# One block of meta rows, values on both halves of a bank, and other engine orders at a handover in a hybrid decoder kernel

## What is computed

```python
p = rms_norm(x, norm_w) @ w_in          # columns: attention q|k|v|gate, HGRN q|f|i|gate
att = sink_attention(qa, [meta k; window k; new k], [meta v; window v; new v], mask, sinks)
S, o = hgrn_chunk(S0, silu(qh), (1-lb)*sigmoid(-fh), ih, log(lb+(1-lb)*sigmoid(fh)))
y = x + concat([att * silu(ga), rms_norm(o) * silu(gh)]) @ w_out
# sample attention, all in one softmax with a sink column:
keys = concat([meta_k (8,16,2,64), buf_k (8,128,2,64), k])      # per sequence its own 16 meta rows
vals = concat([meta_v, buf_v, v])
```

## Time and profile before

| | us |
|---|---|
| median of 3 runs | 1149.72 (1148.98 to 1150.73) |
| the profiled execution | 1151.39 |
| its span, first to last instruction | 1149.5 |
| TensorE busy | 1117.0 |
| VectorE / ScalarE / GpSimd busy | 712.8 / 438.5 / 360.8 |
| TensorE busy in 550 to 560, 560 to 570 | 8.30, 7.40 of 10 |

### The profile page before, as it was taken

The page is one execution under the profiler, slowest core; times in us unless marked ns, Lnnn a source line. Parts: engine busy times, 40 slices in busy tenths (PEclk is TensorE's granted clock), DMA queues, the critical chain, the costliest instruction groups (busy, mean ns, idle before and its releaser), DMA issues.

```text
span 1149.5 us, 25865 instructions
## 1 busy us (share of the span) xinstructions
PE 1117.0 (97%) x9394; PEld 919.2 (80%) x9394; DVE 712.8 (62%) x1849; ACT 438.5 (38%) x1258; POOL 360.8 (31%) x421
## 2 busy tenths in 40 slices
PE   6999999999999999999889999999999999999998
PEld 4877888888888888888676888888888887678887
DVE  6657666666666666667864556655665666755443
ACT  6402222222222222224323565655576665523320
POOL 0003333333333333333531223322332236532331
PEclk9989999999999999999998999999999999999999
DMA  8531111111111111106331611121111134434431
GB/s 286 183 111 57 66 66 64 64 55 64 64 64 64 64 64 64 45 26 242 109 102 39 230 46 55 50 78 46 56 68 63 46 110 159 144 147 152 151 136 74
DMA packets 49391, 108.33 MB, mean 94 GB/s; under 512 B 5088, under 2 KB 17888, under 8 KB 49312
## 3 DMA queue, kind: packets, MB, share of 16 engines
q1 hardware_dynamic: 49328, 107.51, 26.2%
HBM read 70.23 MB, written 38.26 MB: 94 GB/s over the span
## 4 chain that ended last, share of the span: by engine, by line
PE 86%; DVE 6%; POOL 4%; issue 2%; ACT 1%; DMA 1%; DVEq 0%; SPq 0%; POOLq 0%; ACTq 0%
PE h_bank_b L919 5%; PE h_bank_a L919 5%; PE h_bank_b L921 5%; PE h_bank_b L920 5%; PE h_bank_a L921 5%; PE h_bank_a L920 5%; PE o_bank L2641 4%; PE o_bank L2643 4%; PE o_bank L2642 4%; PE h_bank_t L903 4%; PE a_bank_b L1917 3%; PE a_bank_b L1919 3%; PE a_bank_b L1918 3%; PE a_bank_a L1917 3%; PE a_bank_a L1919 3%; PE a_bank_a L1918 3%
## 5 line engine op out<-in xcount | busy, mean ns | idle before, releaser
L1705 DVE CUSTOM_DVE_ANT_0 a_sm<-a_sc,a_hidden,a_neg_sink 128x272 f32<-128x272 f32 x128 | 57.7, 488 | 83.5 <-PE a_sc L1946 83.4
L919 PE MATMUL h_bank_b<-h_w_hi,h_h_hi 128*128 128x512 f32 x256 | 106.4, 416 | 0.1
L919 PE MATMUL h_bank_a<-h_w_hi,h_h_hi 128*128 128x512 f32 x256 | 103.1, 403 | 0.0
L921 PE MATMUL h_bank_b<-h_w_hi,h_h_lo 128*128 128x512 f32 x256 | 100.8, 394 | 0.0
L920 PE MATMUL h_bank_b<-h_w_lo,h_h_hi 128*128 128x512 f32 x256 | 100.2, 391 | 0.0
L921 PE MATMUL h_bank_a<-h_w_hi,h_h_lo 128*128 128x512 f32 x256 | 99.9, 390 | 0.0
L920 PE MATMUL h_bank_a<-h_w_lo,h_h_hi 128*128 128x512 f32 x256 | 99.7, 389 | 0.0
L1917 PE MATMUL a_bank_a<-a_w_hi,a_h_hi 128*128 128x512 f32 (+1 forms) x208 | 77.5, 373 | 0.5 <-DMA a_h_lo<-h_split 0.5
L1917 PE MATMUL a_bank_b<-a_w_hi,a_h_hi 128*128 128x512 f32 (+1 forms) x200 | 76.3, 382 | 0.0
L1501 ACT ACTIVATE a_prb<-a_sm,a_neg_m 128x256 f32<-128x256 f32 x128 | 64.2, 502 | 27.7 <-DVE a_neg_m L1705 25.8
L1919 PE MATMUL a_bank_a<-a_w_hi,a_h_lo 128*128 128x512 f32 (+1 forms) x208 | 73.6, 354 | 0.0
(11 more groups left out here) (328 smaller groups left out, 3048.4 us busy)
## 6 DMA issues: line engine op xcount, KB each, us to landing
h_split<-h_h_hi SPq DMA_DIRECT2D x17, 512.0 KB, 3.0
h_split<-h_h_lo SPq DMA_DIRECT2D x17, 512.0 KB, 3.8
a_h_hi<-h_split SPq DMA_DIRECT2D x17, 512.0 KB, 3.5
a_h_lo<-h_split SPq DMA_DIRECT2D x17, 512.0 KB, 4.4
h_x<-x_prompt SPq DMA_DIRECT2D x16, 512.0 KB, 3.4
o_m<-mixed SPq DMA_DIRECT2D x16, 512.0 KB, 4.1
o_x<-x_prompt SPq DMA_DIRECT2D x16, 512.0 KB, 4.3
y_prompt<-o_x SPq DMA_DIRECT2D x16, 512.0 KB, 2.6
```

The costliest lines, as they stand in the source:

```text
L919: pe.matmul(out[:, :], h_hi[t.slot][:, k, :], hi, start=(k == 0), stop=False)
L921: ins = pe.matmul(out[:, :], h_lo[t.slot][:, k, :], hi, start=False, stop=(k == KT - 1))
L1705: ins = dve.tensor_tensor_reduce(SM[j % 2][:, i, :], sc[:, i, 0:KEYS], hidden[:, mask, :], -SCALE, neg_sink[:, h:h + 1], ALU.add, ALU.min, ...
```

## The change

Five things are changed. The meta keys and values of all 8 sequences are loaded as one block of 128 rows; one transpose takes the place of eight, and one matmul the place of eight, with the probabilities spread by a mask (s_block, s_pm) so that each sequence sees its own 16 rows. The products with the window values go in turn to partitions 0 to 63 and 64 to 127 of the bank, and VectorE adds the halves. The orders of VectorE, GpSimd and ScalarE in the handover are others: more and smaller pieces, k_stats and q_stats apart from k_norm and q_norm, keys_values(0) ahead of weight splits, o_rstd of the last tile ahead of the memsets, three reciprocals behind the copy of KTW. The last tile's far_copy moves from VectorE to ScalarE, and its state product behind half a projection. In tile 1 of attention square_q, q_stats, q_norm and q_split come earlier.

```diff
--- before.py
+++ after.py
@@ -393,14 +393,10 @@
             yield
-            k_levels(last, 2, 3)
+            k_levels(last, 2, 4)
             o_rstd(TILES - 2)
             yield
-            k_levels(last, 3, 4)
-            yield
-            k_levels(last, 4, 5)
-            yield
-            k_levels(last, 5, 6)
+            k_levels(last, 4, 6)
             yield
...
@@ -458,6 +454,14 @@
                 ins.then_inc(o_squared, 1)
+            def far_copy(t):
+                act.wait_ge(lev_mm, 8 * t.n)
+                act.wait_ge(o_mm, t.n)
+                for j in (0, 2):
+                    act.activation(A[32 * j:32 * j + 32, :, 32 * j + 32:32 * j + 64],
+                                   far[32 * j:32 * j + 32, 0:P].rearrange("p (h c) -> p h c", h=HH), ACT.Copy)
+                act.activation(A[0:64, :, 64:P], far[0:64, P:3 * P].rearrange("p (h c) -> p h c", h=HH), ACT.Copy).then_inc(far_copied, 1)
...
@@ -543,6 +547,7 @@
             yield
+            far_copy(last)
             k_copy(last.n)
...
@@ -868,27 +873,28 @@
             g_mul(last)
+            yield
             block_totals(last)
...
             yield
+            q_levels(last, 3, 5)
+            yield
             state_step(before)
             o_var(before.n)
-            q_levels(last, 3, 4)
+            yield
             wait(dve, mix_stored, 16 * before.n)
...
             yield
-            q_levels(last, 4, 5)
-            yield
             q_levels(last, 5, 6)
+            yield
             near_mask(last, 1)
...
             q_levels(last, 7, 8)
-            far_copy(last)
             yield
...
@@ -1204,12 +1211,15 @@
         KW, VW = sb("kw", [P, NS, KVH * HD]), sb("vw", [P, NS, KVH * HD])
-        KM, VM = sb("km", [META, NS, KVH * HD]), sb("vm", [META, NS, KVH * HD])
+        KM, VM = sb("km", [NS * META, KVH * HD]), sb("vm", [NS * META, KVH * HD])
         KTW = sb("ktw", [P, NS, P + META])
-        QZ, PZ, PZM = sb("qz", [P, 72 * NS]), sb("pz", [P, 72 * NS]), sb("pzm", [META, 72 * NS])
+        QZ, PZ, PZM = sb("qz", [P, 72 * NS]), sb("pz", [P, 72 * NS]), sb("pzm", [P, 64])
         s_sink, s_neg, s_m = sb("s_sink", [64, 1]), sb("s_neg", [64, 1]), sb("s_m", [64, 1])
...
         s_p = sb("s_p", [64, P + META])
+        s_block, s_pm = sb("s_block", [64, NS]), sb("s_pm", [64, NS * META])
         s_o = sb("s_o", [64, KVH * HD])
...
@@ -1307,9 +1317,9 @@
             sp.dma_start(KW[:, :, :], win_k.rearrange("b s c -> s b c")).then_inc(cache_loaded, 16)
-            sp.dma_start(KM[:, :, :], meta_k.rearrange("b s c -> s b c")).then_inc(cache_loaded, 16)
+            sp.dma_start(KM[:, :], meta_k.rearrange("b s c -> (b s) c")).then_inc(cache_loaded, 16)
             sp.dma_start(VW[:, :, :], win_v.rearrange("b s c -> s b c")).then_inc(cache_loaded, 16)
-            sp.dma_start(VM[:, :, :], meta_v.rearrange("b s c -> s b c")).then_inc(cache_loaded, 16)
+            sp.dma_start(VM[:, :], meta_v.rearrange("b s c -> (b s) c")).then_inc(cache_loaded, 16)
             sp.dma_start(hidden[:, :, :], masks).then_inc(sink_loaded, 16)
...
@@ -1407,21 +1417,21 @@
             pool.wait_ge(before["g_proj"], TILES)
+            k_rstd_of(tile(0, 0))
             pool.memset(KTS[:, :, :, :].bitcast(F32), 0.0).then_inc(buffers_zeroed, 1)
-            k_rstd_of(tile(0, 0))
             yield
...
             q_rstd_of(tile(0, 0))
+            yield
             pool.wait_ge(sink_loaded, 3 * 16)
             q_weight(tile(0, 0))
-            yield
             q_rstd_of(tile(0, 1))
+            yield
             q_weight(tile(0, 1))
...
             pool.memset(PZ[:, :], 0.0)
-            pool.memset(PZM[:, :], 0.0)
             pool.memset(VMD[:, :], 0.0)
...
@@ -1534,9 +1544,8 @@
             yield
-            split_weights(2, range(0, 4))
             keys_values(tile(0, 0))
-            split_weights(2, range(4, 6))
+            split_weights(2, range(0, 6))
             yield
...
@@ -1578,9 +1587,9 @@
             exps(t0, 0)
+            square_q(t1)
             place_p(t0, 0)
             exps(t0, 1)
-            square_q(t1)
             place_p(t0, 1)
...
@@ -1748,44 +1757,47 @@
             k_stats(tile(0, 0))
-            split_weights(1, range(2, 4))
+            yield
             dve.wait_ge(knw_loaded, 2 * 16)
...
             place_v(tile(0, 0))
-            split_weights(1, range(4, 8))
+            split_weights(1, range(2, 8))
             dve.tensor_scalar(neg_sink[:, :], sink[:, :], -1.0, None, ALU.mult).then_inc(sink_negated, 1)
...
             k_stats(tile(0, 1))
+            yield
             k_norm(tile(0, 1))
...
             q_stats(tile(0, 0))
+            yield
             q_norm(tile(0, 0))
...
             yield
+            q_stats(tile(0, 1))
             split_weights(2, range(4, 8))
             yield
-            q_stats(tile(0, 1))
             q_norm(tile(0, 1))
             yield
-            gate_plus(tile(0, 0))
-            for i in range(4):
-                gate_recip(tile(0, 0), i)
-            gate_mul(tile(0, 0))
-            yield
-
+            q_split(tile(0, 1))
             dve.wait_ge(sq_turned, 1)
             dve.wait_ge(buffers_zeroed, 2)
+            dve.tensor_reduce(s_block[:, :], ident[0:64, 0:64].rearrange("p (b h) -> p b h", h=AH), AX.X, ALU.add)
             for kv in range(KVH):
...
             ins.then_inc(sq_placed, 1)
-            q_split(tile(0, 1))
+            gate_plus(tile(0, 0))
+            gate_recip(tile(0, 0), 0)
             dve.wait_ge(sk_turned, 1)
...
             dve.tensor_copy(KTW[:, :, P:P + META], bank_o[:, 0:NS * META].rearrange("p (b k) -> p b k", k=META)).then_inc(sk_placed, 1)
+            for i in range(1, 4):
+                gate_recip(tile(0, 0), i)
+            gate_mul(tile(0, 0))
...
@@ -1796,33 +1808,38 @@
             dve.wait_ge(s_exped, 1)
+            dve.tensor_tensor(s_pm[:, :].rearrange("p (b k) -> p b k", k=META),
+                              s_p[:, P:P + META].unsqueeze(1).to_broadcast([64, NS, META]),
+                              s_block[:, :].unsqueeze(2).to_broadcast([64, NS, META]), ALU.mult).then_inc(s_step, 1)
             dve.tensor_tensor(s_den[:, :], s_sum[:, :], s_e[:, :], ALU.add).then_inc(s_step, 1)
-            dve.wait_ge(s_step, 4)
+            dve.wait_ge(s_step, 5)
             dve.reciprocal(s_rden[:, :], s_den[:, :]).then_inc(s_step, 1)
...
             dve.tensor_copy(PZ[:, :].rearrange("p (b c) -> p b c", c=72)[:, :, 0:AH], pt[:, 0, 0:64].rearrange("p (b h) -> p b h", h=AH))
-            dve.tensor_copy(PZM[:, :].rearrange("p (b c) -> p b c", c=72)[:, :, 0:AH],
-                            pt[0:META, 0, 64:128].rearrange("p (b h) -> p b h", h=AH)).then_inc(sp_placed, 1)
+            dve.tensor_copy(PZM[:, :], pt[:, 0, 64:128]).then_inc(sp_placed, 1)
             t0, t1 = tile(0, 1), tile(0, 2)
...
             dve.wait_ge(s_pv, 1)
-            dve.wait_ge(s_step, 5)
-            dve.tensor_scalar(s_o[:, :], bank_o[0:64, 0:KVH * HD], s_rden[:, 0:1], None, ALU.mult).then_inc(o_normed, 1)
+            dve.tensor_copy(s_o[:, :], bank_o[64:P, 0:KVH * HD]).then_inc(s_step, 1)
+            dve.wait_ge(s_step, 7)
+            dve.tensor_tensor(s_o[:, :], bank_o[0:64, 0:KVH * HD], s_o[:, :], ALU.add).then_inc(s_step, 1)
+            dve.wait_ge(s_step, 8)
+            dve.tensor_scalar(s_o[:, :], s_o[:, :], s_rden[:, 0:1], None, ALU.mult).then_inc(o_normed, 1)
             k_stats(t1)
...
             maxima(t0, 1, 2)
+            q_stats(t1)
             gate_recip(t0, 0)
+            maxima(t0, 2, 2)
+            q_norm(t1)
             gate_recip(t0, 1)
-            maxima(t0, 2, 2)
-            q_stats(t1)
             gate_recip(t0, 2)
-            q_norm(t1)
+            q_split(t1)
             maxima(t0, 3, 2)
...
             gate_recip(t0, 3)
-            q_split(t1)
             gate_mul(t0)
...
@@ -2026,8 +2043,7 @@
                 pe.transpose(sc[:, b // 4, (b % 4) * P:(b % 4 + 1) * P], KW[:, b, :], ident[:, :])
-                ins = pe.transpose(bank_o[:, b * META:(b + 1) * META], KM[:, b, :], ident[0:META, 0:META])
-            ins.then_inc(sk_turned, 1)
+            pe.transpose(bank_o[:, 0:NS * META], KM[:, :], ident[:, :]).then_inc(sk_turned, 1)
             t2 = tile(0, 2)
...
@@ -2044,16 +2060,18 @@
             pe.wait_ge(s_exped, 1)
+            pe.wait_ge(s_step, 4)
             pe.wait_ge(before["s_new"], TILES)
             pe.transpose(pt[:, 0, 0:64], s_p[:, 0:P], ident[0:64, 0:64])
-            pe.transpose(pt[0:META, 0, 64:128], s_p[:, P:P + META], ident[0:64, 0:64]).then_inc(sp_turned, 1)
+            pe.transpose(pt[:, 0, 64:128], s_pm[:, :], ident[0:64, 0:64]).then_inc(sp_turned, 1)
             scores(t1, 0)
...
             for b in range(NS):
-                c = slice(64 * b, 64 * b + 64)
-                pe.matmul(bank_o[0:64, 0:KVH * HD], PZ[:, c], VW[:, b, :], start=(b == 0), stop=False)
```

(27 more changed lines are left out.)

## The result

| | before | after |
|---|---|---|
| median of 5 runs, us | 1149.72 (1148.57 to 1151.51) | 1135.93 (1135.26 to 1137.91) |
| span of the profiled execution, us | 1149.5 | 1133.3 |

The ratio is 0.9879, with a 95% interval of 0.9866 to 0.9893: 13.8 us less, where 14.25 were forecast. The page of after shows the same picture as the earlier trace rows, with 13.7 us less of busy TensorE. TensorE's idle time, span less busy, went from 32.5 to 30.0 us only: most of the gain is work that got cheaper or ran at the higher clock, and not waits that went.

The account below looks back on a forecast made before the run. TensorE, busy 1117.0 of 1149.5 us, was taken as the bound, with holes in the handover to attention. 15.7 us reaching the loop less 1.45 for the clock gave 14.25: 1149.72 to 1135.5 us, range 1131.5 to 1142.5.

Parts of the forecast that it names:

- Orders ahead of the outputs: HGRN-to-attention handover: holes before levels 4 and 5 go, one comes before level 7; last outputs 3.8 us earlier.
- step 2: TensorE's way to level 4: VectorE's levels are ready, the 0.75 hole goes, start 560.65 instead of 563.15, 2.5 us.
- The weight splits: VectorE's two groups of four before the last outputs: taken at 3.95 and 3.2 us, between 2.72 and 4.50.
- rival A: VectorE bounds the handover: split groups 4.50 each, powers 1 us late, second slow stretch; gain 9.9, 1139.8; chance 0.22.
- Meta rows as one block: Transposes before the sample's scores: 9 of one shape in 1.0 us instead of 3.3, so 2.3 us go.
- Values: Sample's value matmuls: 9 on both halves take 1.7 us; with chunks at full clock, 11.65 to scores(1) becomes 4.5.
- Rival B: Sample's values stay at 0.36 us a matmul and the clock falls there as now; gain 9.7, 1140.1; chance 0.12.
- Into the loop: Attention loop entry: the 2.06 us wait for GpSimd's q_rest goes, exps(3) transposes 15.8 us earlier; 15.7 reach the loop.
- Clock: Holes of 2.4 and 1.0 before the gate's last chunks bring one low-clock stretch, charged at 1.45 us.
- D: Clock falls in the new holes at 571 and stays down until the loop: slower, 1154.2; chance 0.03.
- C: Handover with fewer holes, no slow stretch, values 1.3, splits 2.72 each: gain 17.8, 1131.9; chance 0.13.

Follow-up runs that it names:

- e9: The changed kernel itself, unaltered, run and profiled a second time: 1136.59 us, ratio 0.9891 to the kernel before.
- e1: The changed kernel with the sample's edits (meta rows, values) taken back, so only the engines' orders and far copy on ScalarE: 1144.22 us, 0.9948 of the kernel before.
- e2: The kernel before with only the sample's edits (meta rows as one block, values on both halves), all orders as before: 1143.82 us, ratio 0.9940.
- e3: The kernel before with TensorE's small instructions reordered only: all window transposes then all meta ones, products likewise: 1146.26 us, ratio 0.9965.
- e4: The changed kernel with all eight window products on partitions 0 to 63, without VectorE's copy and sum: 1138.31 us, 0.9896 of the kernel before.
- e5: The changed kernel with square_q, q_stats, q_norm and q_split of attention's tile 1 back where they stood before: 1139.39 us, 0.9905 of the kernel before.
- e7: The changed kernel with ScalarE's gate(0) ahead of the copy of h_kn and VectorE's gate reciprocals earlier: 1134.40 us, 0.9865 of the kernel before.
- e10: The kernel of e7 run and profiled again: 1135.82 us, ratio 0.9880 to the kernel before.
- e12: The changed kernel with the last tile's far copy back on VectorE, behind its last level: 1136.08 us, ratio 0.9883 to the kernel before.
- e6: The changed kernel with VectorE making level 7's queries before near_mask and near_sum, and weight splits before q_stats: 1136.47 us, 0.9883 of the kernel before.
- e8: The changed kernel with the two orders of e6 and e7 together: 1135.20 us, ratio 0.9869 to the kernel before.
- e11: The kernel of e8 run and profiled again: 1134.77 us, ratio 0.9876 to the kernel before.

## Why the prediction was right, step by step

The forecast times stood on the scale of the profile of before; to compare, 2.31 us are added to the rows of after (the difference where the handover begins).

| step | forecast | measured + 2.31 |
|---|---|---|
| turn_k(0) | 553.3 | 553.42 |
| level 4 | 560.65 | 561.27 |
| level 5 | 564.2 | 565.08 |
| level 7, behind its hole | 573.3 | 574.11 |
| last outputs, with the clock's 1.45 | 579.45 | 580.03 |
| sample's scores | 592.1 | 592.80 |
| turn_q(1) | 597.2 | 597.73 |
| scores(1) | 605.9 | 606.13 |
| first transpose of exps(3) | 619.05 | 619.39 |

**Orders ahead of the outputs.** The holes before levels 4 and 5 went, turn_k came 1.4 earlier, and a hole named by VectorE took their place before level 7: 2.06 and 0.82 for the 2.4 and 1.0 forecast. Mis-sized was TensorE's way to level 6, which saved 5.45 us, not 6.5. From turn_k to level 6 the steps had 14.1 us, and 15.0 were measured: 0.3 is a wait for a level that step 2 put at none, and the rest is TensorE's own pieces, added up too short. It cost little, since VectorE was the later one at level 7. The outputs kept 1.8 us in after and 3.4 in e9, for 3.8 less 1.45 forecast. So the steps from level 4 to the sample's scores were 0.6 to 0.9 us late, and the smaller hole before turn_q(1) (1.45 for 1.9) and the cheaper values made up for it: that the end is off by only 0.3 is in part luck.

**The weight splits** on which rival A rested took 3.94 and 2.74 us, for 3.95 and 3.2. Timeline of VectorE in after, and of GpSimd beside the second group:

```profile
564.75 3.94 DVE L1752 SCALAR_TENSOR_TENSOR a_w_lo<-a_raw,c_nw,a_w_hi 128x512 fp32r<-128x512 f32 x4
...
572.46 2.74 DVE L1752 SCALAR_TENSOR_TENSOR a_w_lo<-a_raw,c_nw,a_w_hi 128x512 fp32r<-128x512 f32 x4
```

```profile
572.63 2.07 POOL L1392 TENSOR_TENSOR a_qrstd<-a_qvar,c_half_power 128x8 f32<-128x8 f32 x1 [5.14 <-DVE a_qvar L1676]
```

The second group has a GpSimd power of 2.07 us almost wholly beside it and lost nothing (2.74, for 2.72 beside a still GpSimd in the earlier trace rows). Beside the first group GpSimd had 2.88 us of levels and q_weight, and 1.2 were lost. What GpSimd lost is less clear: its next level, begun at 574.67 beside the group's end, took 1.33 us where the like took 0.43. Rival A fell with this: of the holes that VectorE makes in after, only the two about level 7 are over 0.5 us. By the rule of whole-instruction exclusion (the Trainium skill, SBUF — State Buffer, shared port pair) the groups would have come to 5.6 and 4.8 us; the trace doesn't agree.

**Meta rows as one block.** 2.3 forecast; from the outputs to the scores after is 12.77 and e1, without it, 15.09: 2.32. That this hits the forecast is partly chance, as e1 has 0.4 us of low clock in it and after a new wait of 0.41; the rows themselves give 2.4, since the nine transposes start 0.90 us before the next chunk in after and the 16 start 3.3 before it in e1. What the prediction didn't say is that this term hangs on the orders: e2 kept 0.25 of it, as expected before that run.

**Values.** The sum had 1.7 us, with 1.3 as the lower bound; 4.09 to scores(1) less 2.76 for the chunks is 1.33. The forecast was too careful by 0.4, because it took a value between the rows for alternating halves (1.3) and for one half (2.2). e3 and e4 show two separate effects: 0.36 falls to 0.24 a product without the change of shape, and to 0.12, start to start, with the two halves in turn. That a change of mode drains TensorE and that different tiles work in parallel is what the Trainium skill says (TensorEngine Tiling (Array Packing), Key Properties); e3 and e4 agree with it, with 0.12 and 0.11 us a product. Rival B, values still 0.36 apart, fell. Its half on the clock fell too: it doesn't drop behind the values in any profile without the alternation.

**Into the loop.** The wait for a_qs went, and the stretch saved 1.54 us (forecast 15.8 less 14.1, 1.7). e5 confirms the 1.5; the fall of the clock behind it there is in none of the three other profiles with that wait.

**Clock.** One fall was charged at 1.45 us; in after it cost 1.58 against e9, which had none with the same instructions. Eight profiles have these two holes, with the same orders up to the outputs but for e12's far copy (after, e1, e4, e5, e7, e9, e10, e12): against e9's 10.04 they are 0 to 2.4 us longer, 1.7 in the mean. The prediction took its 1.45 from the fall at 570.3 of before, and there it had cost nothing: e2 and e3 run the same orders with the clock at 1.00 in 570 to 580, and TensorE then waits 1.6 us for VectorE before level 6, so that the stretch is 23.57 and 23.56 for 23.56. In after no wait hides it. TensorE's timeline of e2:

```profile
572.46 0.45 PE L949 MATMUL h_far<-h_lv 128*32 128x32 f32 x16 [1.63 <-DVE h_lv L615]
```

Stretch tables of after, e9 and e10:

```profile
570.00:580.00 10.00, 7.38 (x49) 6.25 (x50) 6.19 (x16) 0.91 (x3) 5.19 (x4) 0.83 0.10 33
```

```profile
570.00:580.00 10.00, 7.13 (x52) 5.58 (x51) 8.18 (x20) 0.91 (x3) 5.17 (x4) 1.00 0.05 9
```

```profile
570.00:580.00 10.00, 7.13 (x35) 5.38 (x34) 6.91 (x17) 1.38 (x4) 5.17 (x4) 0.67 0.00 0
```

A mean of 0.83 over these 10 us is 2.4 GHz with a part of it at 1.2 GHz; in e10 that part is twice as long. So the term was about right as a mean, not as a fact of each execution. Rivals D (the clock stays down until the loop) and C (no fall, everything at its best) didn't come; e9 has C's missing fall and values, and its handover saved 15.5 of C's 17.8 us.

## What to carry to other kernels

Put small matmuls and transposes of one shape together, and let neighbours go to different halves of a bank; 16 products fell from 0.36 to 0.24 us each by order alone. Price the parts of a change together where one shortens what another makes TensorE wait for: here the shorter transposes alone gave 0.25 us, because TensorE then waited 2.2 us longer for VectorE, and with the new orders some 2. Before a hole is attacked by another order, see whether the releasing engine is idle anywhere ahead of it: where it isn't, as before level 7, the hole only moves.

## What the runs showed that was not expected

The same instructions with the same hole are followed by a fall of the clock in one execution and by none in another: behind 2.06 us before level 7 the cost was 0 in e9, 1.6 us in after and 2.4 in e10 (12.43 for 10.04); behind 3.1 us before the outputs the stretch to the scores took 15.73 in e6 and 12.36 and 12.39 in e8 and e11, where 0.4 is e7's edit. Behind waits at the scores (3.11 in e2, 2.70 in e3) it fell in the one profile of each; behind the 2.06 at a_qs it fell in e5 and not in before, e2 and e3. So a profile of one execution carries some 2 us of the clock's, and two kernels with 1 us between them need stretches compared at the same clock.

Part of that lies far from the change. Between 30 and 100 us the code is the same in all kernels, and the fourteen profiles fall into three groups there: with a mean clock of 0.93 (before, e8, e9, e11) the handover begins at 549.86 to 550.32, with 0.95 (seven) at 548.50 to 548.91, with 0.98 (after, e1, e3) at 547.20 to 547.99. That the clock is the cause of these 2 to 3 us is likely from this, and was not tried. The three profiles of the changed orders that entered late (e8, e9, e11) are also the three with no fall about the outputs; why, the runs don't show, and so the missing fall in e8 and e11 can't be put down to their order. The same stretch of before, of after and of e9:

```profile
30.00:100.00 70.00, 67.45 (x407) 55.03 (x406) 43.03 (x121) 19.46 (x40) 6.61 (x8) 0.93 0.45 144
```

```profile
30.00:100.00 70.00, 67.33 (x478) 54.67 (x477) 43.91 (x123) 20.41 (x42) 7.07 (x9) 0.98 0.46 144
```

```profile
30.00:100.00 70.00, 67.53 (x407) 55.15 (x406) 42.56 (x120) 18.97 (x40) 6.59 (x8) 0.93 0.45 144
```
